# A two-layer decoder step with gathered experts: the planner of its instruction order, rewritten as one merge of three queues

## What is computed

```python
def layer(x, ...):
    h = rmsnorm(x, norm1)
    proj = h @ w_in                      # q, k, v, o, pooling input, gates
    ...                                  # mLSTM heads and causal pooling
    x = x + mix
    x = x + peer_ffn(rmsnorm(x, norm2), ...)
    return x + sigmoid(x @ w_gate) * (p @ w_ple)

def peer_ffn(xb, wq, keys, u_tab, v_tab):
    q = (xb @ wq).reshape(T, 8, 2, 128)
    s = einsum('thcd,chkd->thck', q, keys)
    sv, si = top_k(s, 16)
    cand = sv[:, :, 0, :, None] + sv[:, :, 1, None, :]
    top, sel = top_k(cand, 16)
    gate = softmax(top)
    act = gelu(einsum('td,thkd->thk', xb, u_tab[eidx]))
    return einsum('thk,thkd->td', gate * act, v_tab[eidx])
```

## Time and profile before

| | |
|---|---|
| median of 3 runs | 1790.19 us (1785.57 to 1794.6) |
| the profiled execution: its own time | 1792.79 us |
| its span, first to last instruction | 1790.6 us |
| mean granted TensorE clock | 0.824 |
| busy: PE, DVE, ACT, POOL | 76%, 55%, 39%, 28% |
| moved, mean rate | 687.26 MB, 384 GB/s |

### The profile page before, as it was taken

One profiled execution on the slowest core, in us unless ns is written; L12 is line 12 of the kernel. 1 busy time (PEld: TensorE's weight loads), 2 busy tenths in 40 slices (PEclk: granted clock), 3 DMA queues, 4 the chain that ended last, 5 costly groups with the idle time before them and its releaser, 6 DMA issues. The chain is left out here.

```text
span 1790.6 us, 19308 instructions
## 1 busy us (share of the span) xinstructions
PE 1364.3 (76%) x6310; PEld 501.9 (28%) x6310; DVE 992.0 (55%) x2540; ACT 692.9 (39%) x1965; POOL 498.0 (28%) x532
## 2 busy tenths in 40 slices
PE   7967689788948879757767897898756677777766
PEld 3523134333413333211113433443311211111113
DVE  1373754756883455875443436668874344555443
ACT  2234435334433453333332645343343333333334
POOL 0031232232222223224332222222333133333330
PEclk9968599889979989986668898899877865676678
DMA  7697699999989999999999799999999989999992
GB/s 309 239 375 306 244 426 428 378 399 426 424 349 377 426 427 417 427 387 392 427 426 422 284 418 421 377 422 416 410 349 427 378 342 427 427 427 427 427 427 116
DMA packets 96737, 687.26 MB, mean 384 GB/s; under 512 B 11104, under 2 KB 12640, under 8 KB 14318
## 3 DMA queue, kind: packets, MB, share of 16 engines
q0 software_dynamic: 76032, 553.68, 74.8%
q1 hardware_dynamic: 20606, 132.36, 18.3%
HBM read 679.87 MB, written 6.59 MB: 383 GB/s over the span
## 5 line engine op out<-in xcount | busy, mean ns | idle before, releaser
L1202 PE MATMUL acc<-rows,weighted 128*64 128x512 f32 x2048 | 699.5, 789 | 268.6 <-ACT weighted L1593 257.2
L2068 DVE SCALAR_TENSOR_TENSOR rows<-rows,shown 128x1024 f32<-128x1024 f32 x528 | 632.7, 1220 | 381.5 <-DMA rows<-in_uv,index_B 249.5
L1399 POOL DMA_INDIRECT rows<-in_uv,index_A x256 | 242.4, 947 | 722.6 <-PE acc L1202 585.7
L889 PE MATMUL bank<-wring,turned 128*128 128x512 f32 (+1 forms) x840 | 385.5, 607 | 8.7 <-DMA wring<-in_w 7.7
L1399 POOL DMA_INDIRECT rows<-in_uv,index_B x256 | 240.4, 939 | 496.6 <-PE acc L1202 474.4
L1202 PEld LDWEIGHTS acc<-rows,weighted 128*64 128x64 f32 x2048 | 134.6, 162 | 731.1 <-ACT weighted L1593 619.7
L889 PEld LDWEIGHTS bank<-wring,turned 128*128 128x128 f32 x840 | 157.7, 196 | 207.6 <-issue 197.3
L1582 ACT ACTIVATE dots_B<-dots_B 128x1 f32<-128x1 f32 x256 | 51.6, 202 | 359.8 <-DVE rows L2068 354.6
L1582 ACT ACTIVATE dots_A<-dots_A 128x1 f32<-128x1 f32 x256 | 51.3, 200 | 267.5 <-DVE rows L2068 253.9
L1593 ACT ACTIVATE weighted<-consts,dots_A 128x64 f32<-128x64 f32 x256 | 89.0, 348 | 8.4
L1593 ACT ACTIVATE weighted<-consts,dots_B 128x64 f32<-128x64 f32 x256 | 89.0, 348 | 8.4
(11 more groups left out here) (312 smaller groups left out, 999.6 us busy)
## 6 DMA issues: line engine op xcount, KB each, us to landing
wring<-in_w SPq DMA_DIRECT2D x107, 1024.0 KB
out_sample<-scratch SPq DMA_DIRECT2D x2, 2128.5 KB, 11.9
scratch<-in_c_s SPq DMA_DIRECT2D x2, 2064.0 KB, 16.0
rows<-in_uv,index_A POOLq DMA_INDIRECT x256
rows<-in_uv,index_B POOLq DMA_INDIRECT x256
keys<-in_keys SPq DMA_DIRECT2D x2, 1024.0 KB
gain<-in_gain SPq DMA_DIRECT2D x3, 640.0 KB
consts<-in_consts SPq DMA_DIRECT2D x1, 1243.0 KB, 11.9
```

The lines of the kernel that those rows point to most:

```text
L889: ins = pe.matmul(ps[:, part], turned["A"][:, 4 * h + c, :], w[:, c, part], start=first, stop=end, skip_group_check=True)
L1202: ins = pe.matmul(acc[c * 64:(c + 1) * 64, :], weighted[:, n % STATS, :], row[:, c * BLOCK:(c + 1) * BLOCK], start=first, stop=end, skip_g ...
L1399: pool.indirect_dma_start(out=rows[:, n % RING, :], out_offset=None, in_=a["uv"], in_offset=bass.IndirectOffsetOnAxis(ap=index[kind][:, pa ...
L2068: dve.scalar_tensor_tensor(u, u, 1.0, shown[:, :, :], ALU.mult, ALU.mult, accum_out=dots[kind][:, part, i:i + 1]).then_inc(u_used, 1)
```

## The change

The planner is rewritten; the functions that emit instructions, the stages and their inner order are the same.

- `dots_stream` and `vals_stream` give two queues over all 528 gathers in place of `groups_of`; a `vals` needs only that its `dots` is placed, and `dots` that the shares of its heads are. Both queues run through all phases.
- At each step the heads of the queues (`dots`, `vals`, stages; in phase 0 the ranking steps as a fourth) are costed: model time of begin, plus, for each later step of the entry, the idle that it forces on its engine beyond what the next `dots` or `vals` leaves idle anyway (`until`), weighted 0.7, 0.7 and 0.3 for PE, DVE and ACT. The lowest cost goes first.
- Stages get a bonus of 20 us times the lag of their done share behind the passed share of this pass's `vals` / 0.95, cut to between -1 and 3 us. The ranking queue gets 4 us when fewer than 8 gathers beyond the issued ones have shares, else 0.2.
- `Clocks` models ScalarE's tables (1.3 us a switch, twice for the logarithm), the weight halves as a stream of their own (3.5 us alone, 5 beside rows), and has new costs: `dots` 1.25 and 0.9, `vals` 1.1, row 2.47, issue 1.25, flight 2.7.

```diff
-def groups_of(p):
...
+def dots_stream():
+    out = []
     for g in GATHERS:
         if g[2] == 0:
             out.append(("show", *g[:2]))
         out.append(("dots", *g))
+    return out
+
+def vals_stream():
+    out = []
+    for g in GATHERS:
+        out.append(("vals", *g))
+        if g[2] + 1 == EACH[KIND[g[0]]]:
+            out.append(("place", *g[:2]))
     return out
@@
-PATIENCE = 0.3
-MARGIN = 8.0
-HOLD = 0
-URGENT, URGENT_IDLE, PACE = 8, 0.5, 0.8
-ROW, HALF_LOAD, ISSUE, FLIGHT, SIGNAL = 2.5, 2.5, 1.0, 3.0, 0.1
+ROW, ALONE, SHARED, ISSUE, FLIGHT, SIGNAL, TABLE = 2.47, 3.5, 5.0, 1.25, 2.7, 0.1, 1.3
+TABLES = {"turn": "sqrt", "turn2": "sqrt", "gates": "log", "weigh": "exp", "state_args": "exp", "sample_args": "exp", "norm_heads": "sqrt",
+          "soften": "exp", "gate": "sigmoid", "final": "sqrt", "dots": "gelu"}
+WEIGHT = {"PE": 0.7, "DVE": 0.7, "ACT": 0.3}
+EARLY_BY, PULL, MOST = 0.95, 20.0, 3.0
+AHEAD, RUSH = 8, 4.0
@@
+    def run(self, e, until=None):
...
         for engine, us in self.steps(e):
             if engine == "PE":
                 now = max(now, self.banks[0])
+            if engine == "ACT" and table and self.table != table:
+                us += TABLE * (2 if table == "log" else 1)
             begin = max(at[engine], now)
+            if start is None:
+                start = begin
+            else:
+                cost += WEIGHT[engine] * max(0.0, begin - max(at[engine], until[engine])) if until else 0.0
             at[engine] = begin + us
             now = begin + us + SIGNAL
+        return at, now, (now if start is None else start) + cost
+
+    def until(self, dots, vals):
+        row = self.run(dots[0]) if dots and dots[0][0] == "dots" else None
+        row = row[2] if row else 0.0
+        return {"DVE": row, "ACT": row + 1.3, "PE": self.first(vals[0]) if vals and vals[0][0] == "vals" and vals[0][1:] in self.dotted else 0.0}
@@
+                begin = max(self.half_dma - 1.0, self.at["PE"] + 1.0)
+                shared = self.dma > begin
+                self.half_dma = begin + (SHARED if shared else ALONE)
+                self.dma = max(self.dma, begin) + ROW
+                self.half_free.append(self.half_dma)
@@
+    for p, (stages, beside, later) in enumerate(phases, -1):
...
+        own = [g for g in GATHERS if p >= 0 and g[0] in PASS_TILES[p]]
+        ranked = [e for e in stages if e[0] in RANKING] if beside else []
...
+        while ranked or plain or beside or later or (stages is phases[-1][0] and (dots or vals)):
+            heads = [(q, 0.0) for q in (dots, vals) if q and ready_for(q[0], placed)]
...
+            if able:
+                heads.append((ranked, RUSH if clocks.left() < AHEAD else 0.2))
+            front = plain or beside or (later if not ranked else [])
+            if front and not waits(front[0]):
+                passed = sum(("vals", *g) in placed for g in own) / max(1, len(own))
+                behind = PULL * (passed / EARLY_BY - done / total)
+                heads.append((front, max(-1.0, min(MOST, behind))))
+            until = clocks.until(dots, vals)
+            found = [(clocks.cost(q[0], until), bonus, q) for q, bonus in heads if fits(q[0])]
+            found = [(cost - bonus, i, q) for i, (cost, bonus, q) in enumerate(found) if cost is not None]
+            chosen = min(found)[2].pop(0)
```

More of the change, by code:

```diff
@@ L303, in ready_for @@
         return ("norm", t, "turn2") in placed
[L304 to L309, removed]
+    if kind == "dots":
+        return (("turn_s", t) if KIND[t] == "S" else ("prob", t, head_of_gather(t, group[3]))) in placed
+    if kind == "vals":
+        return ("dots", *group[1:]) in placed
     return True
@@ L385, in issue, with known, left @@
             self.landed.append(self.dma)
-        return None
-    def known(self, n):
+    def known(self, n, stage):
         t, part, i = GATHERS[n]
[L391 to L399, removed]
+        return self.done.get(("turn_s", t) if KIND[t] == "S" else (stage, t, head_of_gather(t, i)))
+    def left(self):
+        n = known = len(self.landed)
+        while known < min(len(GATHERS), n + AHEAD) and self.known(known, "turn_prob") is not None:
             known += 1
@@ L413, in first @@
             if half_key(e) != APART:
[L414 removed]
+                ready = max(ready, self.half_free[n - WRING] if n >= WRING else ALONE * (n + 1))
         if stage == "dots":
@@ L427, in steps @@
         out = SMALL[stage] if small and stage in SMALL else STEPS[stage]
-        if stage in ("project", "query", "gate", "mix") and e[{"gate": 3}.get(stage, 3)] == 0:
+        if stage in ("project", "query", "gate", "mix") and e[3] == 0:
             out = out[:1]
@@ L442, in steps, with table_of @@
         return out
-    def run(self, e, for_real, engines=("PE", "DVE")):
+    def table_of(self, e):
+        if e[0] == "project":
+            return "sigmoid" if e[2:4] == (3, 1) else None
+        if e[0] == "norm":
+            return "sqrt" if KIND[e[1]] == "S" else None
+        if e[0] == "gate" and not e[3] or e[0] in ("turn", "turn2", "final") and KIND[e[1]] == "S":
+            return None
+        return TABLES.get(e[0])
+    def run(self, e, until=None):
         ready = self.first(e)
@@ L448, in run @@
             return None
-        at = dict(self.at)
-        now, idle, start = ready, 0.0, None
+        at, now, cost, start, table = dict(self.at), ready, 0.0, None, self.table_of(e)
         for engine, us in self.steps(e):
@@ L498, in opens, with woven @@
     return 1 - e[3] if e[0] in ("project", "mix", "query", "gate") else OPENS.get(e[0], 0)
-def woven(groups, stages, clocks, out, beside=(), later=()):
-    groups, stages, beside, later, waited, half_done = list(groups), list(stages), list(beside), list(later), 0, {}
+def woven(phases):
+    dots, vals, out, placed, clocks, half_done = dots_stream(), vals_stream(), [], set(), Clocks(), {}
     def emit(e):
-        clocks.run(e, True)
+        clocks.take(e)
         out.append(e)
+        placed.add(e)
+        if e[0] == "turn_prob":
+            placed.update(("prob", e[1], h) for h in range(e[2], e[3]))
         dense = e[0] in ("project", "mix", "query", "gate")
@@ L568, in make_schedule @@
+    return out
 def make_schedule():
     first, second = stage_front(0), stage_front(1)
-    ready = 1 + first.index(("turn_prob", 0, 0, 1))
     alone = [e for e in second if tile_of(e) == 1 or e[0] in ("turn", "norm", "gates", "forget", "project")]
```

118 lines of the change are left out of this document (31 added, 87 removed).

## The result

| | before | after |
|---|---|---|
| median | 1787.88 us (1779.8 to 1794.6, 4 runs) | 1839.35 us (1836.82 to 1843.96, 4 runs) |
| span of the profiled execution | 1790.6 us | 1834.7 us |
| mean granted TensorE clock | 0.824 | 0.828 |
| mean rate | 384 GB/s | 375 GB/s |
| transfer time lost, length x (1 - GB/s / 427), in steps of 10 us | 181 us | 225 us |

The ratio is 1.029 [1.024, 1.034]: slower by 51 us, where 50 us of gain was forecast.

The account below looks back on a forecast made before the run. The bytes were taken as the bound: 687.26 MB at 427 GB/s are 1609.5 us, the other 181 us lost. Terms 12 + 8 + 18 + 10 + 5 + 7 - 10 = 50 us gave 1740 us, range 1715 to 1765.

Parts of the forecast that it names:

- What is new: Stops that the new merge makes and the old had not: two small ones, -10 us, bounds 0 and -60.
- The work up to turn_prob(0,0,1) is one queue in both ... nothing: Stretch before the first row gather: same order in both planners, the first 34.6 us of loss stay.
- 130 to 220: At 130 to 220 us: the exponential's lump goes, ranking chains lose less; gain 18 us, bounds -8 and 33.3.
- Boundary 980 to 1030: Gate halves in a row at 980 to 1030 us: landed products begin first; gain 12 us, bounds 0 and 15.8.
- Boundary 1410 to 1450: Gate halves, then a wait for emb: products placed ahead of embed cover part; gain 8 us, bounds 0 and 14.1.
- Ranking stretches: 510 to 580, 790 to 810, 1290 to 1330 us: more dots between VectorE's work; gain 10 us, bounds 0 and 30.
- Sample-state stretches: 350 to 390 and 1130 to 1170 us: better mixing; gain 5 us, bounds 0 and 12.7.
- The end: Last 40 us: the last dots run before apply and final of tile 4; gain 7 us, bounds 0 and 14.
- A: Rival: nearly all lost time recovered, the eight middle stretches shrinking by three quarters; 1700 us, chance 0.13.
- C: Rival: the losses move and do not shrink; 1785 us, within 8 either way, chance 0.13.
- B: Rival: finer interleaving lowers TensorE's granted clock until TensorE bounds the dense stretches; 1770 us, chance 0.08.
- D: Rival: pacing makes indices late, stopping GpSimd for up to 20 us at three boundaries; 1805 us, chance 0.14.

Follow-up runs that it names:

- the planner's constant: The changed planner with the slack of place set from 0 to -20 us, so place goes as soon as it can: 1793.26 us.
- the fastest kernel: The changed planner with place slack -20, embed(3) ahead of final(3), show(0,0) out of the prologue and RUSH cut from 4 us to 0.2: 1758.15 us.
- the repaired base: The changed planner with place slack -20, embed(3) ahead of final(3) and show(0,0) out of the prologue, RUSH still 4 us: 1777.01 us.

## Why the prediction was wrong

**The step that failed is "What is new".** It put ten us for two small stops, with 60 as the worst bound, and priced the new order by the kind of stop that the old one had (7.2 and 5.6 us). The change had taken `place` out of a queue in which it stood directly behind its `vals` with rules of its own (`groups[0][0] in ("show", "place")`: taken if it begins up to 0.5 us later) and made it a head that competes by cost. That line is among those removed, and I costed it nowhere. The question to put was the text's own, what is queued behind this entry: all `vals` of the next half. And a bound was at hand: 8 rows of ring are 20 us a stop, at up to ten halves. Measured: 46 us by the planner's constant, 36 us by moving the entries alone, with the misplaced `show(3,0)` as a part of the difference. The stated range was too narrow even for its own terms: all of them moved halfway to their bounds give 1705 to 1799, not 1715 to 1765, the -10 alone 25 us.

**"The work up to turn_prob(0,0,1) is one queue in both ... nothing" was wrong.** The stages are one queue, but `dots_stream` is offered beside it, and its `show` fits. 11 us.

**130 to 220.** In the window itself 14 of the 18 us came: 33.3 lost before, 19.0 after (337 GB/s). But the stops moved to both sides of it. 94 to 240 lost 34.9 us before (325 GB/s) and 31.8 after, 3 less. In the fastest kernel it loses 13.0, 22 less than before. The exponential still stands behind Ln and a table load in it (load at 177.62), so it was not that lump alone. I gave the lift of ranking steps as a help, and as a lower bound of -8 that it could hold the `dots` back. It did the second: it costs 19 us on the repaired base.

**Boundary 980 to 1030.** Right in mechanism: products now run between the gates, 423 GB/s in 980 to 1050, all of the 15.8 us gone where I took 12. One reading was off: GpSimd's 29.18 us ended at 995.79, and 960 to 1010 lost 8.2 us (357 GB/s); the other 7.6 of the 15.8 lay at 1010 to 1030, behind the stop. A stop in 960 to 980 (13.5 us), of the late `place(1,1)` and of `show(3,0)`, took nearly all of it back.

**Boundary 1410 to 1450.** 14.1 before. The wait for `emb` that I named as unknown to both planners was 16.16 us of TensorE in the kernel after, now at 1500, and 13.0 us were lost at 1420 to 1440 besides. I had its cause by half: not only the store, also the one buffer of `emb` holds the load back. In the fastest kernel the wait is still 12.76 us, and 1450 to 1460 loses 6.0. I took 8, and no more than that is shown.

**Ranking stretches.** I took 10 of 30.0. The fastest kernel loses 19.3 (520 to 570) and 11.9 (1350 to 1390), 31.2 together: nothing was gained in the sum. But VectorE's work is not the whole bound. The stretch of the earlier trace rows, 7.2 us lost before, is clean there, and the first has grown from 13.0 to 19.3, with a wait of 13.94 us for `index_B` in it. So the order can help and can harm; why the two losses stay is open.

**Sample-state stretches.** I took a gain of 5, and they lose 23 more in the fastest kernel. Cause open, above.

**The end.** 7 taken. After: 42.9 us lost from 1790 on, 10 more than before (32.5), because the last `place` of tile 4 stood behind eight `dots`. TensorE waits for it 17.78 us, and the products of tile 5 come at 1813.38, behind the 14 us of tile 4's gate halves:

```profile
1793.78 3.38 PE L1210 MATMUL bank<-summed,consts 128*64 128x512 f32 x4 [17.78 <-ACT summed L1602]
...
1813.38 1.93 PE L1196 MATMUL acc<-rows,weighted 128*32 128x256 f32 x32
```

With the place repaired it loses 22.6, 10 less than before.

**The rivals.** A, nearly all recovered, is out: even the fastest kernel loses 149 us. C, the losses move and do not shrink, describes the planner with the place repaired (182 us lost against 181, in new places) and the kernel after but for its 44 us more; it came nearer than the forecast. B, the clock: granted 0.828 after against 0.824; the dense stretch from 240 runs at 0.89 and 424 GB/s. TensorE did not become the bound. D, indices too late: the sign came out right, the mechanism not, and 1805 was too low. It gave one wait of 14.0 us (`index_B`); pacing earlier made the kernel slower, and no pacing at all made a late index real, 65.6 us, where D had feared it from the pacing. The prediction's own test fell too: between the first and the last gather the loss was to stay under 95 us. It is 141 us (1676.7 us from 99.58 to 1776.28 at 391 GB/s); before it was 112.

**What the change was good for** is pacing, 31 us, and tables, 22 us, against three faults of 46, 19 and 11. These do not add up: 53 won and 76 lost would be 23 us slower, and 51 were measured. Pacing and tables were taken out of the fastest kernel only, and may be worth less beside the faults; or the rest of the merge is slower than the old rules. No run tells which; without pacing, the fastest kernel is level with the kernel before. With the three faults mended and `embed` moved (some 5 us of its own), it is 1758.15 against 1789.34 us: 31 us, where I had forecast 50.

## What to carry to other kernels

When the order of a static multi-engine program is a merge by earliest begin, an entry that starts on an engine other than the one it keeps waiting, and that heads a queue of others, must not compete by a cost that grows with its own delay: it starves. And an entry whose real wait the planner does not know, as that of `show` for the readers of its buffer, can be taken far too early. Before building, count from the finished list how far one queue runs ahead of each such entry, and compare that with the depth of the ring. And test each part of a heuristic by itself: in one change there were two parts worth 31 and 22 us and three that lost 46, 19 and 11.

## What the runs showed that I had not expected

- Counting the table load in the planner (1283 ns in the profile) gave 22 us and not one load fewer.
- What a repair is worth depends on the faults that stay: `show` and the ranking lift were worth 30 us with the places repaired and 15 without.
- A stop of GpSimd costs less than it lasts, and by no fixed amount. In the kernel after, waits of 20.71, 21.50 and 24.46 us went with losses of 13.5, 12.2 and 9.0 us; before, 29.18 us with 8.2 (960 to 1010). So the transfers went on for 7 to 21 us of a stop, and not always for the 20 us that eight rows of 2.46 us last.
